# Opening each norm stage with four weight units, and reordering attention, in a four-layer hybrid trunk

## The reference

```
m = silu(cond) @ w_ada + b_ada              # 6 parts of 1024: shift, scale, gate, twice
h = rms_norm(x, g) * (1 + scale) + shift    # for x with c, for z with c_ctx
x = x + gate * mixer(h_x, h_z)
x = x + gate * (silu(a) * b) @ w_out        # a, b = split(h @ w_in), hidden 2816
```

## Time and profile before

| | |
|---|---|
| Median of 3 runs | 2657.54 us (2657.25 to 2658.66) |
| Profiled execution, its own time | 2653.29 us |
| Span of its trace | 2651.5 us, 35653 instructions |
| TensorE busy | 2421.7 us, 91% |
| VectorE, ScalarE, GpSimd busy | 1391.4, 933.2, 1027.3 us |
| Mean granted TensorE clock | 0.976 |
| Read from HBM | 335.80 MB, 128 GB/s over the span |

### The profile page before, as it was taken

How to read it: one execution, slowest core, us unless ns; L and a number is a source line. 1 busy time by engine, 2 the same in 40 slices (tenths; PEclk the granted TensorE clock), 3 DMA queues, 4 the chain that set the end, 5 groups by cost and what they waited for, 6 DMA issues and landing times.

```text
span 2651.5 us, 35653 instructions
## 1 busy us (share of the span) xinstructions
PE 2421.7 (91%) x12016; PEld 1986.7 (75%) x12016; DVE 1391.4 (52%) x2277; ACT 933.2 (35%) x1519; POOL 1027.3 (39%) x431
## 2 busy tenths in 40 slices
PE   0539999999989999998999999999999999987998
PEld 0426677888877877787788887777788887766998
DVE  7996657666142333217766133555766614466441
ACT  2205543322232333324222223554322323354553
POOL 1212233444433333333444433223344443333886
PEclk9869999999999999999999999999999999998999
DMA  7241125555322222224655327222455532223554
GB/s 292 107 181 54 47 64 183 205 190 185 101 83 80 80 80 72 76 90 151 217 194 197 99 84 149 73 81 96 167 200 196 182 95 84 83 64 95 164 184 128
DMA packets 116411, 341.55 MB, mean 129 GB/s; under 512 B 34928, under 2 KB 36208, under 8 KB 115696
## 3 DMA queue, kind: packets, MB, share of 16 engines
q1 hardware_dynamic: 108304, 335.01, 37.7%
q10 hardware_dynamic: 8032, 5.52, 1.4%
HBM read 335.80 MB, written 4.69 MB: 128 GB/s over the span
## 4 chain that ended last, share of the span: by engine, by line
issue 62%; POOL 22%; PE 10%; DVE 3%; ACT 1%; POOLq 1%; DVEq 0%; ACTq 0%
POOL w_lo L462 22%; PE low_banks L469 8%; PE high_banks L469 2%; DVE rot L1561 1%; ACT e_x L1051 1%; DVE ssum_rstd L1379 1%; POOLq L458 0%; POOLq L461 0%; DVE a_x L1616 0%; DVE high_banks L1564 0%; DVE d_st L1588 0%; ACT tmp L934 0%; DVE a_x L1612 0%; ACT lnm L942 0%; DVE xT L1360 0%
## 5 line engine op out<-in xcount | busy, mean ns | idle before, releaser
L462 POOL TENSOR_TENSOR w_lo<-w_raw,w_hi 128x1024 fp32r<-128x1024 f32 x424 | 1026.9, 2433 | 1603.4 <-ACT w_hi L918 1602.8
L469 PE MATMUL low_banks<-h_hi,w_hi 128*128 128x512 f32 (+1 forms) x1728 | 636.7, 368 | 22.0 <-DVE h_lo L1409 13.2
L469 PE MATMUL low_banks<-h_lo,w_hi 128*128 128x512 f32 (+1 forms) x1728 | 626.7, 363 | 0.0
L469 PE MATMUL low_banks<-h_hi,w_lo 128*128 128x512 f32 (+1 forms) x1728 | 626.6, 363 | 0.0
L918 ACT ACTIVATE w_hi<-w_raw 128x1024 fp32r<-128x1024 f32 x424 | 444.2, 1055 | 483.9 <-PE high_banks L469 212.0
L469 PEld LDWEIGHTS low_banks<-h_hi,w_hi 128*128 128x128 f32 x1728 | 331.9, 192 | 82.1 <-DVE h_lo L1409 16.4
L469 PEld LDWEIGHTS low_banks<-h_lo,w_hi 128*128 128x128 f32 x1728 | 332.2, 192 | 50.0 <-issue 1.9
L469 PEld LDWEIGHTS low_banks<-h_hi,w_lo 128*128 128x128 f32 x1728 | 331.8, 192 | 48.9
L1311 DVE SCALAR_TENSOR_TENSOR ssum_rstd<-ada_raw,high_banks 128x1024 f32<-128x1024 f32 x288 | 351.1, 1219 | 24.9 <-DMA ada_raw<-in_ada_w 16.3
L1212 ACT ACTIVATE lnm<-low_banks 128x512 f32<-128x512 f32 (+1 forms) x88 | 47.7, 542 | 407.2 <-PE low_banks L469 407.2
L469 PE MATMUL high_banks<-h_hi,w_hi 128*128 128x512 f32 (+1 forms) x384 | 146.5, 382 | 14.9 <-issue 7.9
(11 more groups left out here) (187 smaller groups left out, 3877.6 us busy)
## 6 DMA issues: line engine op xcount, KB each, us to landing
w_raw<-in_weights SPq DMA_DIRECT2D x424, 512.0 KB, 3.6
ada_raw<-in_ada_w SPq DMA_DIRECT2D x144, 512.0 KB, 3.6
ada_rest<-in_ada_w SPq DMA_DIRECT2D x8, 2048.0 KB, 7.8
ada_first<-in_ada_w SPq DMA_DIRECT2D x4, 2048.0 KB, 14.1
bias<-rpb_skew SPq DMA_DIRECT2D x64, 64.0 KB, 2.4
rpb_skew<-rpb_rows ACTq DMA_DIRECT2D x1, 3556.0 KB, 36.5
cond_l<-in_cond SPq DMA_DIRECT2D x3, 1024.0 KB, 4.5
xT<-in_xT SPq DMA_DIRECT2D x1, 2048.0 KB, 14.0
```

The costliest lines, as they stand in the source:

```text
L462: nc.gpsimd.tensor_tensor(out=w_lo[:, r, :], in0=w_raw[:, r, :], in1=w_hi[:, r, :], op=ALU.subtract).then_inc(lo_ready, 1)
L469: return nc.tensor.matmul(dst, lhsT, rhs, start=start, stop=stop, **kw)
```

## The change

There are five parts.

1. **Openings.** The first two units over the latents and the context are replaced by `opening`, in the four feed-forwards and in the retention's first head. TensorE takes units n and n+1 over latent tiles 0 to 3, then waits for units n+2 and n+3 and takes them over the same tiles, then the latent tiles 4 to 7 of both pairs, with the context's ones-matmul between, then the context of both pairs. On ACT the context's root and `h_hi` are one routine `context`, and the conversion of unit n+3 stands ahead of it. The latents' root stands ahead of the conversion of n+1, and the conversion of n+2 goes in between the latent tiles. The lists on VectorE follow. The latents' ones-matmul moves to the middle of the first context half of the stage before.
2. **Feed-forward.** Output tiles 0 to 3 use banks 0 to 3, and 4 to 7 use banks 4 to 7. The wait for the modulation stands before the second half; the 48 products are planned as eleven rounds of four and a last four. The first step of the first half goes over output tiles 0 and 1, then 2 and 3, with a wait on `u_free` before each two. The banks of the ones-matmuls alternate with the norm.
3. **Values.** The second half goes into other banks (6, 7, 4, 5), so it waits for no copy; the context's ones-matmul stands behind tile 4.
4. **Differential attention.** K's unit is split six tiles and two; the transposes of the tile before (`turn`) stand between, the product with V (`weighted`) behind. VectorE takes the maxima right after K's rotation, the first two ahead of the sub-norm; ACT takes the exp of bank 0 between the sub-norm's Exp and `y_hi`. In layer 3 the sub-norm has banks 4 and 5, and TensorE takes three tiles of the next Q unit ahead of the scores. Neighbourhood attention keeps its order.
5. **Projection.** `turn` and `weighted` of the last tile stand apart, with two tiles of unit 2 between; tile 7 of units 0 to 3 goes last, back to back.

The core of the diff:

```diff
-ADA_TRIPS = ((2, 6), (9, 4))
+ADA_TRIPS = ((11, 4),)
+ADA_LAST = 4
+V_BANKS = ((0, 1, 2, 3), (6, 7, 4, 5))
+K_FRONT = 6
+Q_AHEAD = 3
-MS_BANK = (7, 6)
+MS_BANKS = ((3, 4), (7, 6))
...
+            def opening(n, q, context):
+                front, rear = range(KT // 2), range(KT // 2, KT)
+                take(n + 1)
+                rows(n, bank[0:2], 0, front, q)
+                take(n + 3)
+                if context and q % 2 and z_tiles(q + 1) > z_tiles(q) + 2:
+                    pe.wait_ge(x_new[1], z_tiles(q + 1) - 2)
+                rows(n + 2, bank[2:4], 0, front)
+                last = rows(n, bank[0:2], 0, rear, q)
+                if not context:
+                    last.then_inc(unit_used, 2)
+                    rows(n + 2, bank[2:4], 0, rear).then_inc(unit_used, 2)
+                    return
+                square_sum(q, 1)
+                rows(n + 2, bank[2:4], 0, rear)
+                rows(n, bank[0:2], 1, range(KT), q).then_inc(unit_used, 2)
+                rows(n + 2, bank[2:4], 1, range(KT)).then_inc(unit_used, 2)
...
+                        if k == KT // 2 and q:
+                            square_sum(q, 1)
...
-                pe.wait_ge(L.v_act, 2)
-                pe.wait_ge(L.v_dve, 2)
...
+                def tile_da(t, slot, place):
+                    if L.zq and place >= 2:
+                        pe.wait_ge(L.y_ready, t - 1)
+                    ahead = 0 if L.zq or place == 0 else Q_AHEAD
+                    unit(t * 2 + n, slot, bank[6], H, L.W, tiles=range(ahead, KT)).then_inc(unit_used, 1)
...
+                    unit(t * 2 + (n + 1), slot + 1, bank[7], H, TOK, tiles=range(K_FRONT))
+                    if place >= 1:
+                        turn(t - 1)
+                    unit(t * 2 + (n + 1), slot + 1, bank[7], H, TOK, tiles=range(K_FRONT, KT)).then_inc(unit_used, 1)
...
+                        weighted(t - 1, o_bank)
+                    if not L.zq and place < 3:
+                        pe.wait_ge(L.qk_dve, t * 2 + 1)
+                        unit(t * 2 + (n + 2), slot + 2, bank[6], H, L.W, tiles=range(Q_AHEAD))
...
+                    for j in range(L.banks):
+                        score(j)
+                        if j == 1 and place >= 1:
+                            mean_square(t - 1, ms_bank)
...
-                    last_back()
-                    part(2, range(3))
+                    last_turn()
+                    part(2, range(2))
+                    last_weighted()
+                    part(2, range(2, 5))
...
-                    for s in range(3):
+                    for s in range(4):
                         part(s, (KT - 1,)).then_inc(unit_used, 1)
-                    part(3, range(3, KT)).then_inc(unit_used, 1)
...
-                if ada:
-
-                    pe.wait_ge(ada_done, MOD * (li + 2))
...
+                    banks = bank[4 * half:4 * half + 4]
+                    if half and ada:
+                        pe.wait_ge(ada_done, MOD * (li + 2))
...
+            def context(q, L, units):
+                conv(units + 3)
+                root(q, 1)
+                for m in range(KT):
+                    high(q, L, m, 1)
             def after_feed_forward(q, L, units):
                 for m in range(4, KT):
                     stream_square(q, m, 0)
-                stream_square(q, 4, 1)
                 root(q, 0)
+                conv(units + 1)
+                for m in range(3):
+                    high(q, L, m, 0)
+                conv(units + 2)
+                high(q, L, 3, 0)
+                for m in range(4, KT):
+                    stream_square(q, m, 1)
+                    high(q, L, m, 0)
+                context(q, L, units)
...
+                def tile_da(t, place):
+                    if place:
+                        weights_(t - 1)
...
+                    rotate(bank[7][:, 0:SEQ], kT[:, 0:SEQ], 2).then_inc(L.qk_dve, 1)
+                    maxima(t, 0, range(2))
+                    if place:
+                        subnorm(t - 1, da_banks(L)[0])
+                    maxima(t, 0, range(2, L.banks))
+                    if place:
+                        low(t - 1, da_banks(L)[0])
```

More of the change, by code:

```diff
@@ L494, in _, with rows @@
             H = (h_hi, h_lo)
-            def stream_unit(n, slot, dst, q, c, tiles=range(KT)):
+            def rows(slot, banks, c, tiles, q=None):
                 for k in tiles:
-                    pe.wait_ge(h_ready[c], q * KT + k + 1)
-                    last = unit(n, slot, dst, H, TOK if c else SEQ, tiles=(k,), at=SEQ * c)
-                return last
[L504 to L511, removed]
+                    if q is not None:
+                        pe.wait_ge(h_ready[c], q * KT + k + 1)
+                    for g, b in enumerate(banks):
+                        last = three(b[:, COLS[c]], weight(slot + g, k * P, k * P + P),
+                                     (h_hi[:, k, COLS[c]], h_lo[:, k, COLS[c]]), k == 0, k == KT - 1)
+                return last
+            def opening(n, q, context):
[15 more added lines that the diff above has]
+                rows(n + 2, bank[2:4], 1, range(KT)).then_inc(unit_used, 2)
             def square_sum(q, c):
@@ L601, in values_product, with turn @@
                     return last
[L603 removed]
+                def turn(t):
                     pe.wait_ge(L.a_ready, t + 1)
@@ L1090, in finish, with tile_na @@
                         rsqrt(L.W, bank[ms_bank][:, 0:L.W], 2 * DA_DIM, L.ors_ready)
+                        if between is not None:
+                            between()
                         act.wait_ge(L.y_ready, t + 1)
                         nc.scalar.activation(y, tmp[:, 0, 0:L.W], ACT.Copy).then_inc(L.y_hi_ready, 1)
-                def tile(t, c, i, place, slot):
+                def tile_na(t, c, i, place):
                     if place:
-                        exps(t - 1)
+                        exps(t - 1, range(L.banks))
@@ new lines, in tile_da @@
+                    ahead(c, i)
+                    if place:
+                        high(t - 1, *da_banks(L), lambda: exps(t, (0,)))
+                if L.na:
+                    tile_na(0, n, 0, 0)
+                    tile_na(1, n + 2, 0, 1)
+                    with act.Fori(0, (KT - 2) // 2) as i:
+                        for s in range(2):
+                            tile_na(i * 2 + (2 + s), n + 4 + 2 * s, i, 2)
+                    exps(KT - 1, range(L.banks))
+                    value_rows(KT - 1)
+                    turned(KT - 1)
+                    high(KT - 1, LAST_O, LAST_MS)
+                    return
@@ L1650, in attention, with masked @@
-                tile(0, 0, 0)
-                tile(1, 1, 1)
-                per_tile = (1 + 4 + 1) if L.na else 3 + 4
-                with own.loop((KT - 2) // 2, 2 * per_tile) as i:
+                def masked(t, slot):
+                    dve.wait_ge(bias_in[slot], t * 64 + (128 - 64 * slot))
+                    b = bias[:, slot, :, :, :].rearrange("p h q (r k) -> p (h q r) k", k=GRID_W)
+                    own(V.tensor_tensor(out=b, in0=b,
+                                        in1=na_mask[:, :].unsqueeze(1).to_broadcast([P, 4 * ROWS, GRID_W]),
+                                        op=ALU.add))
+                    maxima(t, slot, range(L.banks))
+                    weights_(t)
```

432 lines of the change are left out of this document (213 added, 219 removed).

## The result

The changed kernel takes 2640.09 us (2637.61 to 2644.09, four runs) where the kernel before takes 2657.57 (2657.25 to 2658.66): a ratio of 0.9937, interval 0.9922 to 0.9951, or 17.5 us faster. The forecast was 2637. The profiled executions stand closer together, 2653.29 and 2640.96: the profile before lay 4.3 us under its median, the one after .9 above.

What follows compares the result with a forecast made beforehand. TensorE, busy 91% of 2651.5 us, was taken as the bound, with gains only in its gaps. The terms summed to -20.6 from 2653.3, giving 2632.7; with 4.25 added for the median, 2637 us, range 2605 to 2658.

Steps and rivals of the forecast that it cites:

- second products: Feed-forward second products: waits for the modulation (-5.3) and for `tmp` (-5.4 with restart) go, .9 returns; -9.8 us.
- layer 0's tiles: Layer 0's attention tiles: earlier maxima and exps shorten the period from 20.98 to 20.0 us over seven intervals; -6.9 us.
- layer 2's head: Layer 2's norm and values gain some 5 us, but tile 0's transposes follow the bias chain; 0.
- The openings: Openings of layers 0 to 2, retention included: TensorE waits for the fourth unit's `w_lo`; +14.2 us, the least sure term.
- the projections: Attention projections of layers 0, 2 and 3: split turn saves wait, back-to-back k7 tiles cost some; -1.3 us together.
- The first rival: Openings work as meant, the fourth unit ready in time, 30 us back instead of 14 lost: 2593; chance .12.
- The third rival: Openings of layers 0 to 2 stay at half clock, costing 48 us instead of 14.2: 2671; chance .10.
- Layer 3's tiles and head: Layer 3's attention: tile period falls from 16.12 to 14.3 us, -11.7; its head, norm and values, -5.1.
- The second rival: Attention gains nothing: maxima ahead of the sub-norm delay `tmp`, and 18.6 us come back: 2655; chance .14.
- The start: Start to layer 0's first scores: TensorE comes sooner but waits longer for `kT`, behind `amp`; 0.

Runs made afterwards that it cites:

- the later fourth unit: The changed kernel, but TensorE waits for units n+2 and n+3 only after all eight latent tiles and the context's ones-matmul; 2607.83 us, ratio 0.9815.
- the softmax run: The changed kernel with differential attention's old order back: maxima behind the sub-norm's low part, all exps behind `y_hi`; 2664.10 us, ratio 1.0027.

## Why the prediction was right, and where it was wrong

The time was right, 2637 against 2640; the sum of the terms, -20.6, stands against -12.3 in the profiled executions and -17.5 in the medians. So the sum was 8 us too hopeful, and 5 of these don't show in the time because the two profiled executions fell on different sides of their medians: that the time came within 3 us is in part luck. Three terms were off by 3 us or more: the second products and layer 0's tiles gave too little, layer 2's head more than forecast.

**The openings: right in mechanism, their size less sure.** Forecast was a wait of 8.1 us for `w_lo` and the context's ones-matmul 10 us later; the wait is 7.68, 7.08, 5.96 and 7.68 us, and in layer 0 the context's ones-matmul starts 410.18 - 336.06 = 74.1 us after the last scores instead of 404.47 - 341.42 = 63.1, so 11 us later.

```profile
404.47 0.76 PE L469 MATMUL high_banks<-ssum_rstd,ones 128*128 128x256 f32 x1 [3.11 <-DVE ssum_rstd L1389]
...
410.18 0.59 PE L482 MATMUL high_banks<-ssum_rstd,ones 128*128 128x256 f32 x2
```

The first of these lines is from before, the second from after. With the projections, 15.3 us were forecast and 13.7 measured. The cause was the place of the conversion against the place where TensorE asks: moving the asking gave 32 us. The first rival, an opening that works, is thus real, but in another order of TensorE. Undoing the openings gave 6.5 by medians and some 9 in the stages of its trace, not 14. The retention is where it gave least: from the end of layer 0's second product to the retention's first ones-matmul the kernel before takes 86.8 us, the changed one 91.7 and the one with the openings undone 91.1. There TensorE's time without work is 8.3 us instead of 11.8, but the granted clock is .89 over that stretch instead of .93 (.94 before), so what the shorter waits gave was lost in clock. Why the clock fell more there stays open.

**The clock.** The third rival (the stage stays at half clock) didn't come: the windows show .89 to .92, no whole stage at the lower level of 1.2 GHz. Those of the later fourth unit, over the same four openings, show 1.00 three times, with waits of at most 1.9 us in them. Two readings of the earlier trace rows in the prediction were off. The window at .89 is the retention's opening and no feed-forward's, so layer 2's was not among the three. And .11 of its 46 us is 5.1 us of lost clock, so 10 us at the lower level, not some 7. Neither enters the sum.

**The second products: the step that failed.** -9.8 was forecast, +.5 came. The step was that the wait for the modulation, moved to the second half, leaves nothing late: -5.3 for that wait. The first products did get shorter, by 3.9 us in the three layers, where -5.4 was forecast. The second products, their waits counted in, got 4.4 us longer: at the first half's output tiles 2 and 3 TensorE now waits 2.2 us for the last `tmp`, where it had waited 1.8 for the last product.

```profile
647.10 2.37 POOL L475 TENSOR_TENSOR w_lo<-w_raw,w_hi 128x1024 fp32r<-128x1024 f32 x1 [6.10 <-ACT w_hi L987]
...
647.94 1.54 DVE L1397 TENSOR_TENSOR mod<-ada_sum,bias_ada 128x4 f32 x1 [0.26 <-DVE ssum_rstd L1389]
649.60 0.69 DVE L1864 TENSOR_TENSOR tmp<-low_banks,lnm 128x512 f32<-128x512 f32 x1
...
650.35 0.50 PE L482 MATMUL low_banks<-u_hi,w_hi 128*128 128x512 f32 x1 [2.20 <-DVE tmp L1864]
```

Ahead of that `tmp` on VectorE stand the last round's products and the addition that closes them. I asked who waits for the products, and not what is queued behind them on their own engine. Two runs show it: with the round moved, the wait goes; with the addition alone moved, .8 at most is left. The addition has four columns (eight in its last instance here), and over this stretch its durations in ns are, minimum, median and maximum:

```profile
L1397 DVE TENSOR_TENSOR mod<-ada_sum,bias_ada x6: 164/1249/2077, 604.0 to 663.1; 128x4 f32 x5, 128x8 f32<-128x8 f32 x1
```

**Layer 2's head: wrong, -3.4 instead of 0.** Norm and values gain 5.9 us to the scores of tile 0, near the 5 that I gave them. I let tile 0's transposes take all of it back, since they follow the bias chain, and so took that chain as fixed. But it is issued behind the context's `h_hi`, so it moves with the norm; the table left at 1604.44 in a stage that began 4.2 us later than before, against 1601.16, so 1 us sooner in it, and landed in 34.3 us instead of 36.5. Why the transfer took 2.2 us less stays open; in the nine runs that issue it at this place it took 33.9 to 37.0 us. That the chain is the bound was right: tile 0's transposes waited 2.35 for `n_z`, and with the table sooner that wait went.

```profile
1659.51 0.41 PE L603 MATMUL low_banks<-ident,n_x 128*128 128x128 f32 x2 [2.35 <-DVE n_z L1667]
```

**Layer 0's tiles: -3.9 for -6.9.** The period came out at 275.60 - 255.35 = 20.25 against 20.0, and I took all seven intervals before as 20.98, where the first two were 19.48 and 20.76. The same seven intervals took 141.2 to 142.6 us in other runs that leave them as they are, so the -3.9 is good to about 1 us. What is late next was named rightly, K's rotation. K in one piece, with K's context copied sooner on ACT, removes that wait and brings the period to 19.59; so the split with its order of copies costs here.

```profile
255.35 1.13 PE L482 MATMUL low_banks<-kT,qT 64*128 64x512 f32 x4 [0.65 <-DVE kT L1632]
...
275.60 0.70 PE L482 MATMUL low_banks<-kT,qT 64*128 64x512 f32 x2 [0.66 <-DVE kT L1632]
```

**Layer 3's tiles and head: right.** 2331.18 - 2316.67 = 14.51 against 14.3; -11.4 for -11.7, and -5.8 for -5.1.

```profile
2316.67 0.70 PE L482 MATMUL low_banks<-kT,qT 64*128 64x512 f32 x2 [0.53 <-DVE kT L1632]
...
2331.18 0.70 PE L482 MATMUL low_banks<-kT,qT 64*128 64x512 f32 x2 [0.52 <-DVE kT L1632]
```

The second rival (the order gains nothing) is refuted by the softmax run: the order is worth 24 us in the changed kernel, more than the 18.6 of the forecast. That K's split leans on it, since the transposes then wait 21.5 us for `a`, is likely but not shown: no run has the old order with K in one piece.

**The start: right.** 1.4 us sooner at 194.84, and the wait there grew from 33.4 to 38.9, still for `kT`.

```profile
194.84 2.93 PE L482 MATMUL low_banks<-kT,qT 64*128 64x512 f32 x6 [38.88 <-DVE kT L1632]
```

## What to carry to other kernels

Before a consumer is given more units at once, read from the producer's own list when the last of them can be ready: against the kernel with the old openings, the four-unit opening cost 6.5 us or gave 26, depending on whether TensorE asked for the fourth unit at the fourth or after the eighth tile. When a wait is moved, look at what stands behind the awaited work on its own engine as well as at who waits for it. And an instruction whose work is tiny is not cheap when it is in line ahead of what the bound engine needs.

## What the runs showed of the hardware

That addition of four columns took .16 us alone and up to 2.08 where POOL computed a low half; at 647.94 it ended with the low half, at 649.48 against 647.10 + 2.37 = 649.47. The Trainium skill's page "SBUF — State Buffer", section "SBUF: two separate sides", says that a VectorE instruction with two SBUF inputs that meets a running GpSimd instruction which reads SBUF is blocked until that ends; the trace agrees. What I had not expected is that it would decide a stage through an instruction of that size.

A stretch at half clock follows some waits of about 2 us and not others of the same length: after the wait of 2.2 us for `tmp` the granted clock over the first half of the second product was .97 in layer 0 and 1.00 in layers 1 and 2, and layer 0's took 1.6 us longer. Which layer that falls in changed between runs of kernels that don't differ there: in the run of the later fourth unit it was layers 1 and 2. A difference of 1 to 2 us in one stage of one trace is therefore no proof by itself.

```profile
645.30:709.20 63.90, 61.70 (x265) 50.59 (x264) 18.37 (x31) 15.02 (x15) 28.73 (x12) 0.97 0.42 135
1460.20:1522.60 62.40, 60.20 (x265) 49.47 (x264) 17.72 (x31) 15.03 (x15) 28.77 (x12) 1.00 0.42 138
```
